# Conditioned mLSTM/retention trunk with MoE on 8 cores: eight modulation loads and eighteen weight casts are given other places in the order of work

## The chip, the cores and the metric

The kernel runs on the 8 cores of one Trainium2 chip. Each core works on one of the 8 sequences of the batch, with all weights of its own to read; nothing is exchanged between cores. The metric is the device time in microseconds of the slowest core. Three runs of the kernel before gave 3336.61, 3298.0 and 3298.25 us, with a median of 3298.25 us.

## The reference, cut to what matters

Two layers, each a mixer and then a mixture of experts (MoE). A vector `mod` of six parts per layer is computed from the condition `c` and shifts, scales and gates both halves of the layer.

```python
for l in range(2):
    mod = silu(c) @ w_ada[l] + b_ada[l]            # 1024 -> 6 * 1024
    sh1, sc1, g1, sh2, sc2, g2 = split(mod, 6)
    h = rms_norm(x, norm1_g[l]) * (1 + sc1) + sh1
    # mixer: one input projection, 4 mLSTM heads and 4 retention heads, a branch
    # projection and a sigmoid gate for each, one output projection
    x = x + g1 * hybrid_mixer(h, ...)
    h = rms_norm(x, norm2_g[l]) * (1 + sc2) + sh2
    # 4 groups x 4 experts, top-1 group, top-2 experts in it; 1024 -> 512 -> 1024
    x = x + g2 * hier_moe(h, ...)
return rms_norm(x, final_g)                         # x: 2048 tokens x 1024 per core
```

`w_ada` is 1024 x 6144 f32 per layer. The kernel treats it as 12 pieces of 512 columns, numbered 0 to 11: 0 to 3 make `sh1` and `sc1`, 4 and 5 make `g1`, 6 to 9 make `sh2` and `sc2`, and 10 and 11 make `g2`.

## The kernel before

**Order of work.** The program is straight-line code. A small scheduler (`S.op`, `S.dma`, lines 40 to 159) appends each instruction to its engine's list and puts semaphore waits before it from the buffers that it reads and writes. Each engine works through its own list in order, and so does each issuing engine with its DMAs. Every DMA that POOL issues goes into the one software queue, q0: the loads of the mixer's weights (f32 in HBM, bf16 in SBUF), the loads of `w_ada`, the casts of expert weights, and the scatters and gathers of the MoE. SP and ACT have hardware queues of their own.

**One layer.** A mixer works through two halves of 1024 tokens (`hf` 0 and 1). In each half, `run_stream([0, 1, 2, 3])` computes the four mLSTM heads in 32 slots (4 tasks x 8 chunks of 128 tokens), then `branch_proj(True, 1)` projects them in 8 steps, `run_stream([4, 5, 6, 7])` and `branch_proj(False, 1)` do the same for the retention heads, and `out_gen` does the output projection in 8 steps. That makes 88 slots a half and 176 a layer. In a stream each slot issues, by POOL, one tiny power operation (L782), so POOL keeps step with the stream; in the projections POOL waits only for weight buffers to come free (`load_w`, L501), and in `out_gen` it runs ahead. A stream's V/output-gate products are on L696; the branch projection's two products are on L843 (branch weights in `wq`) and L850 (gate weights in `wk`). `branch_proj(False, 1)` also loads the output weights, eight pieces of 256 KB, at its first two steps.

**Modulation pieces.** `ada_gen` (L866) runs beside the first stream of a half in layer 0. For each piece, POOL loads 512 columns of `w_ada` (2 MB f32 read, 1 MB bf16 written, L276) into one of two halves of `yT`, which is free at that time; PE multiplies them with silu(c) (`ada_mm`, L283, 8 products), ACT copies the row out, and PE turns it back to columns (`ada_tr`, L292). The load of piece p+2 is issued when piece p has been used. Pieces 0 to 3 of layer 0 come before the first mixer (L336). In half 0 of layer 0, pieces 4 to 11 of layer 0 are computed (8 of them), and in half 1 all 12 pieces of layer 1. In layer 1 there are none.

**Casts of the experts' weights.** The 16 experts of a layer are turned from f32 (`w_exp`) into bf16 (`ws`) in HBM beforehand, in 6 DMAs an expert (1 MB read, 512 KB written each), 96 a layer. `precast_slot` is called once in each of the 176 slots and issues (slot x 96 + 167) // 168 in all, so 0.571 a slot, with the last at slot 168.

**MoE.** After a barrier of all engines and DMAs, SP issues the prefetch of the first four experts (24 loads of 512 KB from `ws`, L994) into `ring`. Routing works on four groups of 512 tokens (`ssq`, `modul`, `router_mm`, `to_tokens`, `routing`): the normalized tokens go to `htok[0..3]` (ACT, L1088), routing computes their places, and POOL scatters each `htok` twice to HBM (L1174, 8 DMAs a group). `to_tokens` of the next group writes the same four `htok` buffers and so waits until the scatters that read them have landed. Each `S.op` in ACT's list behind that wait, the next group's `h32k` (L1064) among them, waits too. A second barrier ends the routing; then 47 blocks of 128 rows go through their experts (`wmm`, L1318), with `load_w` (L1304) bringing further experts, and rows are gathered back.

Of the kernel before, what the change touches and what calls it, by code (L numbers as in the profile page):

```python
# [23 lines left out]
RING = 4  # L24
# [172 lines left out]
def build(stop_after=None, dumps=()):  # L197
# [37 lines left out]
    with ExitStack() as st:  # L235
        S = Sched(nc, st)
# [38 lines left out]
        def ada_load(l, jg, dst, buf, extra=()):  # L275
            S.dma("pool", lambda h: h.dma_start(out=dst, in_=W_ADA[l, :, jg * 512:(jg + 1) * 512].rearrange("(k p) n -> p k n", p=128)),  # L276
                  writes=[buf] + list(extra))

        def ada_mm(l, jg, wa_, buf, bk, row, b_row):
            def mm(h):  # L280
                ins = None
                for k in range(8):
                    ins = h.matmul(bank[bk][0:1, :], lhsT=csilb[:, k:k + 1], rhs=wa_[:, k, :], start=(k == 0), stop=(k == 7))  # L283
                return ins
            S.op("pe", mm, reads=[buf, b_c], writes=[pb[bk]])
            S.op("act", lambda h: h.activation(out=row[0:1, :], in_=bank[bk][0:1, :], func=AF.Copy), writes=[pb[bk], b_row])
# [44 lines left out]
        with ExitStack() as p0:  # L331
# [3 lines left out]
            for jg in range(4):  # L335
# [5 lines left out]
                 reads=[b_c], writes=[b_c])  # L341
            S.op("dve", lambda h: h.tensor_scalar(out=csil[:], in0=csil[:], scalar1=0.5, scalar2=None, op0=ALU.mult),
                 reads=[b_c], writes=[b_c])
# [13 lines left out]
                 writes=[b_r])  # L357
# [11 lines left out]
            for t in range(16):  # L369
                S.dma("sp", lambda h, t=t: h.dma_start(out=xs[t % 4][:], in_=X[t * 128:(t + 1) * 128, :]), writes=[b_xs[t % 4]])  # L370
                for hb in range(2):
# [8 lines left out]
                    if eng == "act":  # L380
# [3 lines left out]
                            reads=[], writes=[pb[hb + 2 * (t % 2)], b_xT[t // 4]])  # L384
                    else:
# [3 lines left out]
                            reads=[], writes=[pb[hb + 2 * (t % 2)], b_xT[t // 4]])  # L389
# [14 lines left out]
        if stop_after == "p0":  # L404
            return finish(nc, S, st, final_evs, xT, b_xT, bank, pb, ident, FING, cb, mhalf, OUT, sbt)

        b_ws = [Buf("ws%d" % i) for i in range(2)]
        PCH = 6
        pc_next = [0, 0]

        def precast(l, n):
            for _ in range(n):
                i = pc_next[l]
                if i >= 16 * PCH:
                    return
                pc_next[l] = i + 1
                e, c = divmod(i, PCH)
                cw = EXPW // PCH
                ev = S.dma("pool", lambda h: h.dma_start(out=WS[l][e, :, c * cw:(c + 1) * cw], in_=W_EXP[l, e, :, c * cw:(c + 1) * cw]),
                           track=b_ws[l])  # L420
                b_ws[l].w = ev

        pc_slot = [0, 0]

        def precast_slot(l):

            pc_slot[l] += 1
            precast(l, (pc_slot[l] * 16 * PCH + 167) // 168 - pc_next[l])

        def run(*gens):  # L430

# [10 lines left out]
        for l in range(2):  # L442
            with ExitStack() as mx:
# [49 lines left out]
                for kb in (0, 4, 1, 5, 2, 6, 3, 7):  # L493
                    for j in range(4):
                        S.op("pool", lambda h: h.tensor_scalar(out=dg[:, kb, j, :], in0=identb[:], scalar1=convw[:, l, j, kb:kb + 1],
                                                               scalar2=None, op0=ALU.mult),
                             reads=[b_const, cb["convw"]], writes=[b_dg[kb]])
# [11 lines left out]
                for hf in range(2):  # L509
# [353 lines left out]
                                         reads=[b_tmp], writes=[b_yT[tg]])  # L863
                    def ada_gen():

                        todo = [(0, jg) for jg in range(4, 12)] if hf == 0 else [(1, jg) for jg in range(12)]  # L866
                        np_ = len(todo)
                        at = [3 + p * 28 // (np_ - 1) for p in range(np_)]
                        for p in range(2):
                            ada_load(*todo[p], wav[p], b_wa[p], b_yT if p == 0 else ())  # L870
                        yield
                        p = 0; q = 0
                        for i in range(33):
                            if q < p:
                                ada_tr(*todo[q], mrow, b_mrow, 3)
                                if q + 2 < np_:
                                    ada_load(*todo[q + 2], wav[q % 2], b_wa[q % 2])
                                q += 1
                            if p < np_ and i == at[p]:
                                ada_mm(*todo[p], wav[p % 2], b_wa[p % 2], 3, mrow, b_mrow)  # L880
                                p += 1
                            yield

                    def run_stream(tis, extra=()):
                        stg = {ti: make_stages(tasks[ti]) for ti in tis}
                        seq = [(ti, c) for ti in tis for c in range(8)]
                        n = len(seq)

                        def call(kind, i):
                            ti, c = seq[i]  # L890
                            stg[ti][kind](c, i)
                        extra = iter(extra)
                        next(extra, None)
                        call("A", 0)
                        call("G", 0)
                        for i in range(n):
                            ti, c = seq[i]
                            nxt = tasks[ti + 1] if ti + 1 < 8 else None
                            if c == 0:
                                if ti + 2 < 8 and ti + 2 != 5:  # L900
                                    loads_qk(tasks[ti + 2])
                                if nxt is not None:
                                    loads_vo(nxt)
                                if ti in (3, 7):
                                    branch_proj(ti == 3, 0)
                            precast_slot(l)
                            if i + 1 < n:
                                call("A", i + 1)
                            call("B", i)
                            call("Q", i)  # L910
                            if i >= 1:
                                call("M", i - 1)
                            if i >= 2:
                                call("C2", i - 2)
                            if i + 1 < n:
                                call("G", i + 1)
                            call("T", i)
                            if nxt is not None:
                                w_, t_ = PIECES[c // 2]
                                prologue_piece(nxt, w_, t_, c % 2)  # L920
                            next(extra, None)
                        call("M", n - 1)
                        call("C2", n - 2)
                        call("C2", n - 1)
                        for _ in extra:
                            pass
# [34 lines left out]
                        run((norm_gen(0), 1))  # L961
                    loads_vo(tasks[0])
                    run((gates_gen(), 1), (prologue_gen(), 2))
                    run_stream([0, 1, 2, 3], ada_gen() if l == 0 else ())
                    branch_proj(True, 1)
                    run_stream([4, 5, 6, 7])
                    branch_proj(False, 1)
# [5 lines left out]
            with ExitStack() as mo:  # L973
# [15 lines left out]
                b_wl = [[Buf("wl%d_%d" % (p, i)) for i in range(RING)] for p in range(6)]  # L989
                b_pre = [Buf("wpre%d" % i) for i in range(RING)]  # L990
                b_hsw = [Buf("hsw%d" % i) for i in range(4)]; b_hz = [Buf("hz%d" % i) for i in range(2)]
                for e in range(RING):
                    for p in range(6):
                        ev = S.dma("sp", lambda h: h.dma_start(out=ring[p][:, e, :], in_=WS[l][e, :, p * 2048:(p + 1) * 2048]),  # L994
                                   reads=[b_ws[l]], track=b_pre[e])
                        b_pre[e].w = ev

                def ldreg(h, ap, mx):
                    UID[0] += 1
# [296 lines left out]
                def load_w(b):  # L1296

                    for p in range(6):
                        def f(h):
                            if p == 0:  # L1300
                                KEEP["sp"] = [ldreg(h, btab[b:b + 1, 0:1], 15), ldreg(h, btab[b:b + 1, 2:3], 1), ldreg(h, btab[b:b + 1, 3:4], (RING - 1) * 2048)]
                                KEEP["id"] = nc.next_id()
                            (r0, ev), (r1, cd), (r2, sv) = KEEP["sp"]
                            ins = h.dma_start(out=ring[p][:].rearrange("p a n -> p (a n)")[:, bass.ds(sv, 2048)],  # L1304
                                              in_=WS[l][bass.ds(ev, 1), :, p * 2048:(p + 1) * 2048].rearrange("a p n -> (a p) n"),
                                              cond=cd, bounds_check="skip_entire_dma")
                            if p == 5:
                                free_regs(h, KEEP["id"], [r0, r1, r2])
                            return ins
                        S.dma("sp", f, reads=[b_btab, b_ws[l]] + (b_pre if b < RING else []), writes=[b_wl[p][b % RING]])  # L1310

                def wmm(h, b, out, lhs, p0, n, first, last, insl):

# [69 lines left out]
                for k in range(8):  # L1383
                    S.op("dve", lambda h: h.tensor_scalar(out=dgt[k % 2][:], in0=ident[:], scalar1=modT[:, l, 40 + k:41 + k], scalar2=None, op0=ALU.mult),
                         reads=[cb["ident"], b_mod], writes=[b_dgt[k % 2]])
                    S.op("pe", lambda h: h.matmul(bank[6 + k // 4][:, (k % 4) * 128:(k % 4 + 1) * 128], lhsT=ones32[:], rhs=dgt[k % 2][:], start=True, stop=True),
                         reads=[b_dgt[k % 2], b_const], writes=[pb[6 + k // 4]])
# [60 lines left out]
                for t in range(16):  # L1448
# [4 lines left out]
                    for hb in range(2):  # L1453
# [11 lines left out]
                        else:  # L1465
                            def f(h):
                                for k in range(4):
# [4 lines left out]
                                 writes=[pb[bk + hb], b_fj[hb], b_ft[t % 2]])  # L1472
                    if l == 1:
# [9 lines left out]
                        ev = S.dma("sp", lambda h: h.dma_start(out=OUT[tcs, :], in_=ob[t % 4][:]), reads=[b_ob[t % 4]], track=b_ob[t % 4])  # L1483
# [126 lines left out]
```

How the kernel before makes its waits and increments, by code:

```python
        def thunk():  # L106
            for s, v in waits:
                h.wait_ge(s, v)
            fn(h).then_inc(sem, 1)
# [25 lines left out]
        def thunk():  # L135
            for s, v in waits:
                h.wait_ge(s, v)
            fn(h).then_inc(dsem, 16)
# [16 lines left out]
            def thunk(h=h, waits=waits):  # L155
                for s, v in waits:
                    h.wait_ge(s, v)
```

## Time and profile before

| | |
|---|---|
| runs, us | 3336.61, 3298.0, 3298.25 (median 3298.25) |
| profiled execution, us | 3322.01 |
| its span, slowest core (core 5), us | 3320.0 |
| spans of the 8 cores, us | 3284.4 to 3320.0 |
| PE busy | 2611.8 us, 79% |
| DVE / ACT / POOL busy | 43% / 40% / 20% |
| q0 (POOL's queue), share of 16 DMA engines over the span | 52.4% |
| q1 (SP's queue) | 16.4% |

All times below are microseconds from the start of the span of core 5. Where a view shows a DMA share of 1.00, all 16 DMA engines of the core were working through packets for the whole stretch; somewhat over 1 means that packets overlap. "DMA to landing" is the time from a DMA's issue to its last byte.

### The profile page before, as it was taken

The page shows a single profiled execution, that of the slowest core. Times are in us where ns is not written, and L with a number is a line of the kernel's source. Part 1 is how long each engine was busy: PE and PEld are TensorE (multiplying, and loading weights), DVE is VectorE, ACT ScalarE, POOL GpSimd, SP SyncE. Part 2 cuts the span into 40 slices and gives each one's busy share as a digit, 9 for nine tenths or more (in the row PEclk, how much of TensorE's full clock was granted, in tenths as well). Part 3 has the DMA queues.
Part 4 walks back from the last instruction along what each step waited for, and adds up shares of the span by engine and source line. Part 5 has one row for each costly group of instructions (what it writes and reads, how often), then busy time and mean ns, then how long its engine had stood idle before and what let it go on. Part 6 is the DMA issues. An engine that isn't in the chain of part 4 may idle for free.

```text
span 3320.0 us, 56309 instructions; the slowest of 8 cores (3284.4 to 3320.0 us)
## 1 busy us (share of the span) xinstructions
PE 2611.8 (79%) x13114; PEld 1240.5 (37%) x13114; DVE 1440.6 (43%) x3484; ACT 1314.1 (40%) x2985; POOL 658.1 (20%) x1108
## 2 busy tenths in 40 slices
PE   4787886887798874688956989788988795499977
PEld 3343443343344321344433444333434331144444
DVE  3244273333446333444444555533536433354445
ACT  2465272254447133122224755624736424122224
POOL 0322132022223102000043322311323201100013
PEclk8798998898899987799976999999999998599989
DMA  8399899579989641588662788882779842358857
GB/s 194 55 136 134 116 117 125 70 98 141 132 118 117 101 163 67 174 273 267 214 238 66 112 116 129 116 132 43 113 120 127 124 124 109 115 195 295 269 185 261
DMA packets 186185, 481.55 MB, mean 145 GB/s; under 512 B 19600, under 2 KB 45072, under 8 KB 185488
## 3 DMA queue, kind: packets, MB, share of 16 engines
q0 software_dynamic: 116896, 268.51, 52.4%
q1 hardware_dynamic: 53568, 181.11, 16.4%
q10 hardware_dynamic: 15408, 28.32, 2.9%
q8 instruction: 127, 2.08, 0.3%
q14 instruction: 186, 1.52, 0.2%
HBM read 831.28 MB, written 185.60 MB: 306 GB/s over the span
## 4 chain that ended last, share of the span: by engine, by line
PE 48%; DMA 17%; issue 11%; ACT 9%; DVE 9%; SPq 4%; POOL 1%; another core or an unknown queue 0%; DVEq 0%; ACTq 0%; POOLq 0%
PE bank L1318 9%; PE bank L696 7%; PE bank L843 6%; DMA yT_u<-w_ada 5%; PE bank L850 5%; PE bank L611 4%; DMA wq_u<-w_br 4%; PE bank L942 3%; PE bank L516 2%; DMA ring_u<-ws 2%; SPq L1304 2%; SPq L1001 1%; DMA xs_u<-x 1%; PE bank L1041 1%; PE bank L1066 1%
## 5 line engine op out<-in xcount | busy, mean ns | idle before, releaser
L696 PE MATMUL bank<-wvo_u,hT_u 128*128 128x512 bf16 x2048 | 486.6, 381 | 2.5 <-DMA wvo_u<-w_in 2.5
L1318 PE MATMUL bank<-ring_u,hTb_u 128*128 x1504 | 385.6, 395 | 53.6 <-DMA ring_u<-ws 46.0
L1336 ACT ACTIVATE hTb_u<-bank 128x1024 bf16<-128x1024 bf16 x94 | 96.3, 1024 | 559.0 <-PE bank L1333 487.0
L843 PE MATMUL bank<-ymT_u,wq_u 128*128 128x512 bf16 x1024 | 263.6, 404 | 66.0 <-DMA wq_u<-w_br 54.9
L782 POOL TENSOR_TENSOR tiny_u<-tiny_u,mhalf_u 128x1 f32<-128x1 f32 x256 | 161.8, 632 | 691.4 <-DVE tiny_u L778 389.1
L696 PEld LDWEIGHTS bank<-wvo_u,hT_u 128*128 128x128 bf16 x2048 | 193.7, 98 | 229.5 <-issue 19.1
L853 ACT ACTIVATE pad_u<-bank 128x512 f32<-128x512 f32 x128 | 76.4, 597 | 464.0 <-PE bank L850 464.0
L850 PE MATMUL bank<-hT_u,wk_u 128*128 128x512 bf16 x1024 | 246.8, 385 | 1.8 <-DMA wk_u<-w_in 1.5
L1318 PEld LDWEIGHTS bank<-ring_u,hTb_u 128*128 128x128 bf16 x1504 | 146.5, 100 | 237.2 <-issue 115.7
L1426 POOL DMA_INDIRECT yg_u<-yd,gidx_u x64 | 65.4, 1022 | 715.6 <-DMA yd<-ysb_u 699.4
L1318 PE MATMUL bank<-ring_u,heT_u 128*128 x752 | 178.1, 380 | 10.2 <-DVE heT_u L1365 10.2
L843 PEld LDWEIGHTS bank<-ymT_u,wq_u 128*128 128x128 bf16 x1024 | 103.0, 102 | 201.0 <-issue 94.8
L1376 DVE TENSOR_TENSOR ysb_u<-bank,g2r_u 128x512 f32<-128x512 f32 x188 | 129.4, 689 | 52.0 <-DMA yd<-ysb_u 26.8
L850 PEld LDWEIGHTS bank<-hT_u,wk_u 128*128 128x128 bf16 x1024 | 101.9, 100 | 131.5 <-issue 18.1
L1066 PE MATMUL bank<-h32k_u,wr_s_u 128*20 128x512 f32 x128 | 84.3, 747 | 83.1 <-ACT h32k_u L1064 82.8
L611 PE MATMUL bank<-hT_u,wk_u 128*128 128x512 bf16 x512 | 129.7, 399 | 4.2 <-ACT acc_u L645 4.2
L1351 DVE SCALAR_TENSOR_TENSOR tht_u<-tht_u,bank 128x512 f32<-128x512 f32 x94 | 64.5, 687 | 155.8 <-ACT tht_u L1350 155.5
L855 DVE SCALAR_TENSOR_TENSOR yT_u<-pad_u,bank 128x512 bf16<-128x512 f32 x64 | 44.0, 687 | 200.7 <-ACT pad_u L853 200.7
L611 PE MATMUL bank<-hT_u,wq_u 128*128 128x512 bf16 x512 | 127.3, 394 | 3.7 <-ACT acc_u L645 3.7
L789 DVE SCALAR_TENSOR_TENSOR ymc_u<-bank,tiny_u,gsig_u 128x256 bf16<-128x256 f32 x256 | 122.2, 477 | 4.3 <-POOL tiny_u L782 2.9
L942 PE MATMUL bank<-yT_u,wvo_u 128*128 128x512 bf16 x512 | 121.5, 395 | 1.8 <-DVE yT_u L862 1.8
L699 ACT ACTIVATE vext_u<-bank 128x256 bf16<-128x256 f32 x256 | 96.8, 378 | 60.4 <-PE bank L696 58.3
(259 smaller groups left out, 4620.7 us busy)
## 6 DMA issues: line engine op xcount, KB each, us to landing
ring_u<-ws SPq DMA_DIRECT2D x612, 512.0 KB, 15.6
ws<-w_exp POOLq DMA_DIRECT2D x192, 512.0 KB, 12.5
yd<-ysb_u SPq DMA_DIRECT2D x94, 512.0 KB, 4.8
wvo_u<-w_in POOLq DMA_DIRECT2D x64, 512.0 KB, 10.9
wk_u<-w_in POOLq DMA_DIRECT2D x96, 256.0 KB, 6.8
hblk_u<-hs ACTq DMA_DIRECT2D x88, 256.0 KB, 4.8
yT_u<-w_ada POOLq DMA_DIRECT2D x20, 1024.0 KB, 25.0
xs_u<-x SPq DMA_DIRECT2D x16, 512.0 KB, 9.7
```

The costliest lines, as they stand in the source:

```text
L611: ins = h.matmul(bank[pbi][:], lhsT=wsel[0][wi][:, k, :], rhs=hT[:, k, lc], start=(k == 0), stop=(k == 7))
L696: ins = h.matmul(bank[vb][:], lhsT=hT[:, k, cc], rhs=wvo[wi][:, :, k, :], start=(k == 0), stop=(k == 7))
L699: S.op("act", lambda h: h.activation(out=vext[vi][:, 0:256], in_=bank[vb][:, 0:256], func=AF.Copy), writes=[pb[vb], b_v[vi]])
L782: S.op("pool", lambda h: h.tensor_tensor(out=tny[:, 7:8], in0=tny[:, 4:5], in1=mhalf[:, 0:1], op=ALU.pow), reads=[b_const], writes=[b_tny])
L789: S.op("dve", lambda h: h.scalar_tensor_tensor(out=ymc[vi][:], in0=bank[ob_][:, 0:256], scalar=tny[:, 7:8], in1=gsig[idx % 3][:], op0=ALU. ...
L843: ins = h.matmul(bank[bA][:], lhsT=wq[ji][:, k, :], rhs=ymT[:, k, lc], start=(k == 0), stop=(k == 7))
L850: ins = h.matmul(bank[bB][:], lhsT=wk[ji][:, k, :], rhs=hT[:, k, lc], start=(k == 0), stop=(k == 7))
L942: ins = h.matmul(bank[ob2][:], lhsT=wt[:, k, :], rhs=yT[:, k, lc], start=(k == 0), stop=(k == 7))
L1066: S.op("pe", lambda h: h.matmul(psLT, lhsT=wr[:, k, :], rhs=h32k[k % 2][:], start=(k == 0), stop=(k == 7)), reads=[b_h32k[k % 2], cb["wr"] ...
L1318: ins = h.matmul(out, lhsT=lhs(i), rhs=ring[p][:].rearrange("p a n -> p (a n)")[:, bass.ds(PREG[b][1] + (i % 4) * 512, 512)], start=(first ...
L1336: S.op("act", lambda h: h.activation(out=hT2[b % 2][:].rearrange("p k t -> p (k t)"), in_=psT, func=AF.Copy), writes=[pb[BT], b_hT2[b % 2]])
L1376: S.op("dve", lambda h: h.tensor_tensor(out=ysb[b % 2][:, n * 512:(n + 1) * 512], in0=bank[BY[n]][:], in1=g2r[:, n * 512:(n + 1) * 512], o ...
```

## The change

Three edits. First, the pieces of `w_ada`: half 0 of both layers now computes pieces 4 to 11 of its own layer, and half 1 of layer 0 only pieces 0 to 3 of layer 1. Eight pieces so move from half 1 of layer 0 to half 0 of layer 1; the total stays. Second, only the first 13 experts (78 casts) are cast in the mixer; the other 18 casts are issued by POOL at one go after the prefetch's place at the start of the routing stage, with a tracking buffer of their own (`b_wsl`), so that the prefetch does not wait for them; the MoE's `load_w` does. Third, `precast_slot` counts 2 a slot, but 1 in the 32 slots of the first stream of half 0, and issues (count x 78 + 319) // 320 in all. The count reaches 32 + 144 x 2 = 320 at the last slot.

```diff
-        b_ws = [Buf("ws%d" % i) for i in range(2)]
+
+        b_ws = [Buf("ws%d" % i) for i in range(2)]; b_wsl = [Buf("wsl%d" % i) for i in range(2)]
         PCH = 6
+        PCL = 13 * PCH
         pc_next = [0, 0]
 
         def precast(l, n):
...
                 ev = S.dma("pool", lambda h: h.dma_start(out=WS[l][e, :, c * cw:(c + 1) * cw], in_=W_EXP[l, e, :, c * cw:(c + 1) * cw]),
-                           track=b_ws[l])
-                b_ws[l].w = ev
+                           track=b_ws[l] if i < PCL else b_wsl[l])
+                (b_ws[l] if i < PCL else b_wsl[l]).w = ev
 
         pc_slot = [0, 0]
 
-        def precast_slot(l):
-
-            pc_slot[l] += 1
-            precast(l, (pc_slot[l] * 16 * PCH + 167) // 168 - pc_next[l])
+        def precast_slot(l, wt=2):
+
+            pc_slot[l] += wt
+            precast(l, (pc_slot[l] * PCL + 319) // 320 - pc_next[l] if pc_next[l] < PCL else 0)
...
                     def ada_gen():
 
-                        todo = [(0, jg) for jg in range(4, 12)] if hf == 0 else [(1, jg) for jg in range(12)]
+                        todo = [(1, jg) for jg in range(4)] if l == 0 and hf == 1 else [(l, jg) for jg in range(4, 12)]
...
-                            precast_slot(l)
+                            precast_slot(l, 1 if hf == 0 and tis[0] == 0 else 2)
...
-                    run_stream([0, 1, 2, 3], ada_gen() if l == 0 else ())
+                    run_stream([0, 1, 2, 3], ada_gen() if l == 0 or hf == 0 else ())
...
                         b_pre[e].w = ev
+
+                precast(l, 16 * PCH - pc_next[l])
...
-                        S.dma("sp", f, reads=[b_btab, b_ws[l]] + (b_pre if b < RING else []), writes=[b_wl[p][b % RING]])
+                        S.dma("sp", f, reads=[b_btab, b_ws[l], b_wsl[l]] + (b_pre if b < RING else []), writes=[b_wl[p][b % RING]])
```

## Rows read from the trace of the kernel before

**Rows 1.** The page: busy engines, and the chain that ended last, by line.
```profile
PE 2611.8 (79%) x13114; PEld 1240.5 (37%) x13114; DVE 1440.6 (43%) x3484; ACT 1314.1 (40%) x2985; POOL 658.1 (20%) x1108
...
PE bank L1318 9%; PE bank L696 7%; PE bank L843 6%; DMA yT_u<-w_ada 5%; PE bank L850 5%; PE bank L611 4%; DMA wq_u<-w_br 4%; PE bank L942 3%; PE bank L516 2%; DMA ring_u<-ws 2%; SPq L1304 2%; SPq L1001 1%; DMA xs_u<-x 1%; PE bank L1041 1%; 
```

**Rows 2.** Stretches: stretch, its length, busy us by engine, PE clock, DMA share, GB/s.
```profile
158.00:402.00 244.00, 202.67 (x1040) 96.42 (x1039) 92.83 (x277) 113.46 (x296) 60.35 (x119) 0.93 0.99 128
694.00:958.00 264.00, 215.81 (x1105) 102.31 (x1103) 93.01 (x283) 116.62 (x299) 65.07 (x124) 0.92 1.01 133
1834.00:2023.00 189.00, 172.46 (x911) 83.75 (x910) 91.51 (x266) 106.90 (x288) 53.93 (x112) 0.98 0.83 120
2304.00:2494.00 190.00, 172.44 (x916) 84.03 (x914) 91.74 (x266) 106.92 (x287) 54.65 (x112) 0.98 0.78 118
```

**Rows 3.** PE's waits, 150 to 340 us, and 340 to 402: total, times, longest.
```profile
PE bank L283 <- DMA yT_u<-w_ada: 22.2, 3, 9.1
...
PE bank L696 <- DMA wvo_u<-w_in: 2.5, 2, 1.5
...
PE bank L843 <- DMA wq_u<-w_bm: 8.2, 1, 8.2
```

**Rows 4.** PE's waits, 690 to 905 us.
```profile
PE bank L283 <- DMA yT_u<-w_ada: 38.3, 6, 12.5
```

**Rows 5.** PE's waits in the four retention branch projections, in order of time.
```profile
PE bank L843 <- DMA wq_u<-w_br: 21.3, 3, 12.1
...
PE bank L843 <- DMA wq_u<-w_br: 10.3, 2, 8.3
...
PE bank L843 <- DMA wq_u<-w_br: 14.8, 4, 8.6
...
PE bank L843 <- DMA wq_u<-w_br: 8.6, 3, 4.0
```

**Rows 6.** Two bursts of six casts with nothing else behind them: layer 0, then layer 1.
```profile
L419 POOL DMA_DIRECT2D ws<-w_exp x6: 515/517/529, 588.8 to 591.4; - x6
...
DMA to landing us min/median/max: 10.3/21.9/33.2
...
L419 POOL DMA_DIRECT2D ws<-w_exp x6: 515/515/529, 2201.0 to 2203.6; - x6
...
DMA to landing us min/median/max: 12.8/20.8/25.7
```

**Rows 7.** Stretches as in rows 2: cast burst, output projection, prefetch, group 0's scatters.
```profile
590.00:625.00 35.00, 30.96 (x118) 13.26 (x117) 10.17 (x15) 10.96 (x17) 4.06 (x8) 0.95 1.00 116
...
1136.00:1178.00 42.00, 40.17 (x186) 17.84 (x184) 18.37 (x26) 2.39 (x4) 0.17 (x1) 1.00 0.12 21
...
1179.00:1220.00 41.00, 29.49 (x84) 8.62 (x84) 10.22 (x21) 22.98 (x36) 0.95 (x1) 0.86 0.90 311
...
1239.00:1252.00 13.00, 7.31 (x32) 2.45 (x32) 3.31 (x9) 8.53 (x13) 8.56 (x8) 0.89 0.42 162
```

**Rows 8.** Timeline of layer 0's routing: first scatter of group 0, then ACT's copies.
```profile
1239.31 1.07 POOL L1174 DMA_INDIRECT hs<-htok_u,sidx_u  x1 [59.35 <-DVE msm_u L1061]
...
1248.61 2.81 ACT L1088 ACTIVATE htok_u<-bank 128x1024 bf16<-128x1024 bf16 x3
1251.61 1.02 ACT L1088 ACTIVATE htok_u<-bank 128x1024 bf16<-128x1024 bf16 x1 [0.20 <-issue]
```

**Rows 9.** The same in layer 1: SP's first issue, the first scatter, ACT's copies.
```profile
2711.06 0.33 SPq L985 DMA_DIRECT2D wr_s_u<-wr  x1
...
2771.91 1.05 POOL L1174 DMA_INDIRECT hs<-htok_u,sidx_u  x1 [59.71 <-DVE msm_u L1061]
...
2781.49 3.71 ACT L1088 ACTIVATE htok_u<-bank 128x1024 bf16<-128x1024 bf16 x4
```

**Rows 10.** Start of the program: four loads of POOL's queue against sixteen of SP's.
```profile
L276 POOL DMA_DIRECT2D wa_u<-w_ada x4: 911/928/1078, 1.6 to 4.4; - x4
...
DMA to landing us min/median/max: 17.7/38.0/60.9
```

## The prediction

> **What bounds the kernel now.** I read the page first. PE is busy 79% of the span, and the chain that ended last lies mostly on PE's products, but two DMAs stand in it with 5% and 4%: the loads of `w_ada` and of `w_br` [rows 1]. So some stretches wait for POOL's software queue. The view by stretches shows which. The same work, an mLSTM stream and its branch projection, takes 244 us in half 0 of layer 0 (8 modulation pieces), 264 in half 1 (12 pieces), and 189 and 190 in layer 1 (none). The DMA engines are full in the first two (0.99, 1.01) and not in the others (0.83, 0.78), and PE's clock falls from 0.98 to 0.93 and 0.92 with the waits [rows 2]. The waits name the cause: PE stood 22.2 us for `w_ada` and 10.7 for weights queued behind it in half 0, and 38.3 in half 1 [rows 3, 4]. The retention projections add four waits for `w_br`, 21.3, 10.3, 14.8 and 8.6 us, 55 in all [rows 5]. A stream of this kind hides about 150 us of DMA; what is piled on top makes it longer.
>
> **Fewer pieces beside layer 0's streams.** DMA time is share times length: 242 and 267 us with pieces, 157 and 148 (mean 152) without [rows 2]. A piece is then (242 - 152) / 8 = 11 or (267 - 152) / 12 = 10 us; I take 10. A cast is bounded by the two bursts: (591.4 + 33.2 - 588.8 - 10.3) / 5 = 5.1 us in layer 0 and, worked the same way, 3.1 in layer 1 [rows 6]; mean 4.1. The 40 slots of such a stretch carried 22.9 casts. With the new counts they carry 32 x 0.244 + 8 x 0.4875 = 11.7 in half 0 and 19.5 in half 1.
>
> A piece also costs PE and ACT something when its data is there. Half 0 is 55 us longer than 189, of which 33 are the waits of rows 3; 22 / 8 = 2.8 us. Half 1 is 75 longer, less 38 of waits; 37 / 12 = 3.1. I take 2.9.
>
> Half 0 of layer 0 keeps 8 pieces but sheds 11.2 casts (46 us at 4.1): 242 - 46 = 196 us of DMA for a stretch of 189 + 8 x 2.9 = 212, a share of 0.92. The queue no longer sets the pace: 244 to 212, **-32**. Half 1 keeps 4 pieces: 152 + 40 - 3.4 x 4.1 = 178 us of DMA in 189 + 12 = 201: 264 to 201, **-63**. Half 0 of layer 1 takes 8 pieces: 157 + 80 - 46 = 191 of DMA in 189 + 23 = 212, share 0.90: **+23**. Its upper bound is what 8 pieces cost now with casts at full pace, +55; the lower is nothing. Sum of the three: -72. The PE, ACT and DVE work of the pieces is only moved and is in the 2.9; g1, the second scale and g2 of layer 1 are needed only in its output projection and later.
>
> **Slower pace elsewhere.** A retention stream of 32 slots carries 15.6 casts in place of 18.3, 11 us less of queue ahead of the first `w_br` load. The eight output weights, 2 MB, still stand ahead of the third. Of the 55 us [rows 5] between nothing and 40 can go; I take **-15**, nearer the low end because the output weights are not moved. The casts that this shifts into the last output projection, 4 of them, cost nothing: the DMA engines stand at 0.12 there [rows 7]. If that cover failed, the barrier would come 4 x 5.1 = 20 us later.
>
> **Eighteen casts at the start of routing.** POOL needs 18 x 0.52 = 9 us to issue them [rows 6] and has nothing else until the first scatter 60 us later [rows 8, 9], so the issuing is free. SP's queue: the 24 prefetch loads fill the engines for 0.90 x 41 = 37 us [rows 7]. They are needed only after the second barrier, so their being slowed costs nothing, and nothing that routing waits for is behind them on SP; the small router weights are issued ahead of them.
>
> What is not free is the software queue. The eight scatters of group 0, issued from 1239.3 on, now stand behind all 18 casts, and ACT's four copies of group 1 into `htok`, done at 1252.6, wait for them [rows 8]. Behind those copies, in ACT's list, is the whole of group 2's modulation, and behind that PE and DVE. The DMA engines have 18c us of casts, c each, and 37 of prefetch to do first. That these add, and do not overlap, is seen at the start of the program: four `w_ada` loads against SP's sixteen loads of `x` land (4.4 + 60.9 - 1.6 - 17.7) / 3 = 15.3 us apart, not 10 [rows 10]. The scatters themselves take 0.42 x 13 = 5.5 us [rows 7] and the last copy 1. So the copies end at 1179 + 18c + 37 + 6.5, later than now by 18c - 30; in layer 1, from 2711.1 to 2785.2 [rows 9], the same 18c - 30. Nothing later makes this up, since group to group is one chain. Before it the queue was empty at that point. With the bounds of rows 6 the delay is 26 us (3.1) to 62 us (5.1) a layer; nothing at all if the prefetch were hidden behind the casts. I take 4.6 in layer 0, nearer its own burst, and 4.0 in layer 1: 53 + 42 = **+95**. Later scatter groups find the queue empty again.
>
> The Trainium skill ("DMA: Bandwidth & Descriptors", section on the anatomy of one SWDGE DMA) fits a DMA of this path as 2.0 us plus bytes over 436 GB/s. For the 1 MB that a cast reads this is an estimate of 2.4 us each in a full queue, by which the delay would be 13 us a layer and the sum -61. The bursts of rows 6 do not bear that rate out.
>
> **Sum.** -32 - 63 + 23 - 15 + 95 = +8 us. The profiled execution took 3322 us, 24 above the median of the runs, 3298. So +8 is 3330 in its terms and **3306** in the median's.
>
> **The rivals.** All times in the median's terms. What this measurement can tell from no change is about 2%, 66 us.
>
> *A, faster: scatters find the queue nearly empty.* The casts run at layer 1's 3.1 us or better and the prefetch hides in their gaps, 56 us in all, over before 1239. For it: layer 1's burst, and the routing stage has empty DMA time before the scatters. Against: the burst of layer 0 at 5.1 with the engines at 1.00 [rows 6, 7]. Then only the mixers' -87 remains: 3211. With the additive rule it needs c under 2.2.
> The Trainium skill's 2.4 us would give 3237; its page "HBM Reference" (Specifications) speaks the other way, giving each core of a streaming pair half of 716 GB/s, an estimate of 4.4 us for the 1.5 MB that a cast reads and writes.
>
> *B, slower: the burst is dearer than any seen.* Place: group 1's copies in both layers. All eight cores cast and prefetch at once, after a barrier that comes at about the same time on each, which no burst of rows 6 did. At 6.5 us a cast the delay is 87 a layer: +174 - 87 = +87, 3385. It decides from 18c - 30 > 76, c over 5.9. Against: 5.1 was already with full engines.
>
> *C, layer 1's first half turns into layer 0's.* The eight pieces there cost the +55 that they cost now, because a piece waits for its own turn in the queue however free the mean is. For: the load of piece p+2 is issued only when piece p is used. Against: the shares of about 0.9 worked out above. Sum +40: 3338.
>
> That the change does not do what it says I exclude by the diff: 96 casts and 24 pieces stay, and the count of 320 gives 78.
>
> **How the numbers follow.** Main case 0.60: its bounds are c from 3.1 to 5.1 in both layers (52 to 124 for routing) and mixers of -75 to -105, so 3245 to 3347. A 0.15, C 0.15, B 0.08, and 0.02 for the mixers gaining nothing. The range is 3240 to 3355; it holds the main case and C and leaves out most of A and B. Faster by over 2% (under 3232) is most of A and a little of the main case's edge: 0.15. Slower by over 2% (over 3364) is B and a little of C: 0.09. Within: 0.76.
>
> **What would show it.** Right: mLSTM stretches of about 212, 201, 212 and 189 us, DMA shares under 0.95 in each, hardly any PE wait for `w_ada`; ACT's second group of `htok` copies ending some 53 and 42 us later after the first barrier than now, with a DMA share near 1 from the barrier to the scatters, and PE idle there. Wrong: copies of group 1 on time (A), casts over 5.9 us apart in routing (B), PE waits of 20 us or more for `w_ada` in layer 1 (C), or a retention projection that waits as long as before.

## The result

The changed kernel took 3358.78 us (median of 5 runs, 3340.53 to 3507.92), the kernel before beside it 3312.8 us. In some runs of either kernel a die shows a lower granted clock and the run is a few per cent longer; the ratios, here and below, leave such runs out. The ratio is 1.0126, 95% interval 1.0065 to 1.0188. So the change costs 21 to 62 us, near 42. The forecast was +8, in a range of -58 to +57.

The profile after shows two large movements that nearly cancel. First the page: PE's and ACT's work is unchanged, and the share of POOL's queue falls from 52.4% to 49.0%.

```profile
span 3356.8 us, 56324 instructions; the slowest of 8 cores (3289.8 to 3356.8 us)
...
PE 2604.0 (78%) x13114; PEld 1239.7 (37%) x13114; DVE 1442.2 (43%) x3484; ACT 1311.8 (39%) x2985; POOL 653.3 (19%) x1108
...
q0 software_dynamic: 116896, 268.51, 49.0%
```

**The mixers gained what was forecast.** Stretches of the changed kernel, columns as in [rows 2]: the four mLSTM streams with their branch projections, then the two stretches from the last output product to the first expert product.

```profile
157.00:369.00 212.00, 199.97 (x1039) 96.86 (x1037) 92.97 (x277) 112.48 (x295) 54.97 (x109) 0.95 0.85 120
652.00:854.00 202.00, 186.73 (x976) 90.59 (x975) 92.07 (x272) 109.77 (x291) 55.15 (x112) 0.97 0.88 123
1794.00:2001.00 207.00, 195.24 (x1038) 95.32 (x1036) 92.86 (x277) 112.52 (x296) 54.35 (x108) 0.98 0.81 123
2283.00:2476.00 193.00, 174.41 (x916) 84.74 (x915) 91.94 (x266) 107.12 (x288) 51.63 (x108) 0.97 0.67 107
1070.00:1321.00 251.00, 96.47 (x306) 28.94 (x306) 68.07 (x234) 65.20 (x98) 42.05 (x51) 0.67 0.63 142
2689.00:2930.00 241.00, 99.65 (x307) 29.94 (x305) 68.58 (x234) 65.30 (x98) 41.98 (x51) 0.66 0.64 147
```

Against 244, 264, 189 and 190 us [rows 2] the four are 212, 202, 207 and 193, with DMA shares of 0.67 to 0.88 where two were full. PE's wait for `w_ada` [rows 3, 4] is gone. Its waits for `w_br`, in order of time, are 39 us in place of 55 [rows 5]:

```profile
PE bank L845 <- DMA wq_u<-w_br: 11.4, 3, 6.8
...
PE bank L845 <- DMA wq_u<-w_br: 8.1, 2, 6.0
...
PE bank L845 <- DMA wq_u<-w_br: 11.8, 3, 8.3
...
PE bank L845 <- DMA wq_u<-w_br: 7.6, 2, 6.9
```

**Routing lost more than that.** The last two stretches were 185 and 184 us on the slowest core before. The timeline of ACT in the changed kernel, layer 0 and then layer 1 (start, length, and in brackets ACT's idle time before), answers to [rows 8, 9]:

```profile
1141.90 0.57 ACT L1081 ACTIVATE lgT_u<-bank 20x512 f32<-20x512 f32 x1
1195.74 1.02 ACT L1092 ACTIVATE htok_u<-bank 128x1024 bf16<-128x1024 bf16 x1 [53.27 <-DMA hs<-htok_u,sidx_u]
1198.46 1.02 ACT L1092 ACTIVATE htok_u<-bank 128x1024 bf16<-128x1024 bf16 x1 [1.70 <-DMA hs<-htok_u,sidx_u]
...
1203.57 1.02 ACT L1092 ACTIVATE htok_u<-bank 128x1024 bf16<-128x1024 bf16 x1 [1.64 <-DMA hs<-htok_u,sidx_u]
...
2811.95 1.02 ACT L1092 ACTIVATE htok_u<-bank 128x1024 bf16<-128x1024 bf16 x1 [49.34 <-DMA hs<-htok_u,sidx_u]
...
2819.78 1.02 ACT L1092 ACTIVATE htok_u<-bank 128x1024 bf16<-128x1024 bf16 x1 [1.64 <-DMA hs<-htok_u,sidx_u]
```

ACT stands for 53.3 and 49.3 us before its first copy of group 1, each time for a scatter, and again 1.4 to 1.7 us before each further one. The DMA engines are full meanwhile and PE is nearly idle (8 of 66 us), at a granted clock of 0.58 of its 2.4 GHz:

```profile
1072.00:1130.00 58.00, 40.98 (x122) 11.25 (x122) 20.77 (x61) 28.69 (x46) 10.29 (x20) 0.90 0.96 158
1130.00:1196.00 66.00, 8.18 (x32) 2.63 (x32) 3.28 (x8) 5.40 (x10) 8.24 (x8) 0.58 0.99 185
```

What the readings below rest on is one table, worked out from the first and last products of each stage in the one trace of each kernel, as the median of the 8 cores. "mL" is an mLSTM stream with its projection, "ret" the same for retention, a and b the two halves, "rout" the stretch from the last output product to the first expert product.

```
                        layer 0                              layer 1
                    mL a  ret a  mL b  ret b  rout     mL a  ret a  mL b  ret b  rout   slowest span
before             243.5  197.1 262.4  187.0 181.8    189.1  192.7 189.8  187.2 183.4    3320.0
after              210.3  188.5 202.4  184.7 240.6    210.5  186.3 192.8  184.1 234.9    3356.8
all in mixer       212.0  192.7 210.6  189.7 181.5    210.5  192.8 192.1  188.5 182.5    3254.2
pieces only        237.9  195.5 205.5  185.3 183.5    232.9  192.6 192.0  187.1 182.3    3324.0
late prefetch      208.8  191.1 202.4  185.0 209.5    209.7  187.8 192.7  184.7 201.2    3287.6
spread             208.8  188.2 202.4  184.7 188.0    210.0  185.5 192.8  184.7 186.3    3228.1
burst of 9         212.1  191.0 202.5  188.0 190.4    208.6  187.9 189.9  187.3 188.6    3254.5
spread, old places 210.4  188.2 248.5  184.0 186.8    189.8  187.7 189.6  184.0 187.3    3257.1
spread 14          212.1  191.3 202.4  185.1 184.2    208.5  186.8 192.2  184.4 184.0    3255.2
```

From before to after, the eight mixer columns sum to -89.2 and the two routing columns to +110.3. A single trace moves by some us without any edit: the spread kernel, traced a second time, gave 190.1 and 188.3 us of routing in place of 188.0 and 186.3.

### The profile page after: what moved, and what is told of

Read it like the earlier page. It is cut to its first block, busy times and chain, and to the rows that moved or that the text cites. A ratio compares the mean times of both kernels' runs of the same rounds, so it can differ in the third digit from the quotient of the medians.

```text
span 3356.8 us, 56324 instructions; the slowest of 8 cores (3289.8 to 3356.8 us)
## 1 busy us (share of the span) xinstructions
PE 2604.0 (78%) x13114; PEld 1239.7 (37%) x13114; DVE 1442.2 (43%) x3484; ACT 1311.8 (39%) x2985; POOL 653.3 (19%) x1108
## 4 chain that ended last, share of the span: by engine, by line
PE 49%; issue 11%; DMA 10%; ACT 10%; DVE 9%; another core or an unknown queue 5%; SPq 5%; DVEq 1%; ACTq 0%; POOL 0%; POOLq 0%
PE bank L698 7%; PE bank L1322 7%; PE bank L845 6%; PE bank L852 6%; PE bank L613 5%; PE bank L944 3%; DMA wq_u<-w_br 3%; DMA yd<-ysb_u 3%; DMA ring_u<-ws 2%; PE bank L518 2%; SPq L1308 2%; PE bank L283 2%; SPq L1005 1%; PE bank L644 1%
## 5 line engine op out<-in xcount | busy, mean ns | idle before, releaser
L1322 PE MATMUL bank<-ring_u,hTb_u 128*128 x1504 | 378.1, 388 | 59.5 <-DMA ring_u<-ws 51.8
L698 PEld LDWEIGHTS bank<-wvo_u,hT_u 128*128 128x128 bf16 x2048 | 193.7, 98 | 222.6 <-issue 10.7
L1070 PE MATMUL bank<-h32k_u,wr_s_u 128*20 128x512 f32 x128 | 88.2, 779 | 190.1 <-ACT h32k_u L1068 189.4
L1178 POOL DMA_INDIRECT hs<-htok_u,sidx_u x64 | 63.9, 998 | 366.2 <-DVE msm_u L1065 313.7
L421 POOL DMA_DIRECT2D ws<-w_exp x192 | 105.9, 554 | 90.9 <-issue 88.5
```

What stands on the lines that cost most here:

```text
L698: ins = h.matmul(bank[vb][:], lhsT=hT[:, k, cc], rhs=wvo[wi][:, :, k, :], start=(k == 0), stop=(k == 7))
L1070: S.op("pe", lambda h: h.matmul(psLT, lhsT=wr[:, k, :], rhs=h32k[k % 2][:], start=(k == 0), stop=(k == 7)), reads=[b_h32k[k % 2], cb["wr"] ...
L1322: ins = h.matmul(out, lhsT=lhs(i), rhs=ring[p][:].rearrange("p a n -> p (a n)")[:, bass.ds(PREG[b][1] + (i % 4) * 512, 512)], start=(first ...
```

## The experiments

**All casts in the mixer.** Undoes the burst alone.

```diff
-        PCL = 13 * PCH
+        PCL = 16 * PCH
```

> All 96 casts stay in the mixer (0.6 a slot, 0.3 beside the eight-piece streams), none at the start of routing; the moved modulation pieces and the half pace stay. Queue theory (the loss is group 1's copies waiting for scatters that stand behind 18 casts): the stretch from the last output product to the first expert product goes back to 184 to 190 us in both layers, 123 us less than in the changed kernel, and the mixers take 5 to 20 us more for the 18 casts; about 3240 us, 55 to 70 below the kernel before. Rival (the mixers' gain comes only from having 18 fewer casts, and the moved pieces give nothing net): mixers as long as before, about 3290 us.

Measured: 3255.24 us (3250.14 to 3262.41), ratio to before 0.9823 (0.9781 to 0.9865). Routing is back at 181.5 and 182.5 us, and the mixers take 29 us more than in the changed kernel for 18 more casts (the eight columns summed), more than the 5 to 20 expected. The rival falls: the mixers stay 60 us shorter than before with all 96 casts in them. Putting 18 casts in a burst turned a gain of 1.8% into a loss of 1.3%.

**The pieces alone.** The kernel before with the `todo` line and the `run_stream` line of the change, nothing else.

```diff
-                        todo = [(0, jg) for jg in range(4, 12)] if hf == 0 else [(1, jg) for jg in range(12)]
+                        todo = [(1, jg) for jg in range(4)] if l == 0 and hf == 1 else [(l, jg) for jg in range(4, 12)]
...
-                    run_stream([0, 1, 2, 3], ada_gen() if l == 0 else ())
+                    run_stream([0, 1, 2, 3], ada_gen() if l == 0 or hf == 0 else ())
```

> The kernel before with the eight modulation pieces moved and nothing else: casts at full pace, all in the mixer. Theory (a stretch is long where its DMA time exceeds what the stream hides): half 1 of layer 0 falls from 264 to 201 to 206 us, half 0 of layer 1 rises from 189 to about 240, as half 0 of layer 0 is now, and half 0 of layer 0 stays at 244; net -10, about 3290 us. Rival (moving the pieces is the whole gain and the pace of casts does nothing): half 0 of layer 1 rises to 212 only, net -40, about 3258 us.

Measured: 0.9954 (0.9914 to 0.9993), some 15 us below before; 3312.52 us as the median of all its 11 runs. Half 1 of layer 0 falls by 56.9 us and half 0 of layer 1 rises by 43.8, close to the theory. Half 0 of layer 0, whose code is the same as before, reads 237.9 us in place of 243.5, so a difference of 6 us in such a full stretch says nothing. The wait for `w_ada` is back in layer 1, in the view of PE's waits there:

```profile
PE bank L283 <- DMA yT_u<-w_ada: 17.6, 2, 10.6
...
PE bank L843 <- DMA wq_u<-w_bm: 2.1, 1, 2.1
```

Against "all in mixer", which differs only in the pace of casts, the two eight-piece stretches are 25.9 and 22.4 us longer. Over the eight mixer columns the moved pieces alone give 20 us (5.6 of them in that unchanged stretch) and the new pace another 40; the pieces need the pace, or their new place fills up as the old one did.

**Prefetch after group 1's copies.** The changed kernel, the burst kept.

```diff
-                for e in range(RING):
+                def prefetch():
+                    for e in range(RING):
...
-                                   reads=[b_ws[l]], track=b_pre[e])
...
+                                       reads=[b_ws[l], b_T1], track=b_pre[e])
...
                 precast(l, 16 * PCH - pc_next[l])
+                b_T1 = Buf("t1")
...
                     to_tokens(g)
+                    if g == 1:
+                        b_T1.w = b_htok[3].w
+                        prefetch()
```

> The changed kernel, with SP's 24 prefetch loads issued only after group 1's copies instead of at the barrier; the burst of 18 casts stays. Theory that casts and prefetch add up on the DMA engines: group 1's copies come 37 us a layer earlier than in the changed kernel, still some 20 us later than before; in all 65 to 75 us less than the changed kernel, about 3280 us. Rival (the scatters wait for the casts alone, and the prefetch runs beside them for nothing): no change, 3350 us. The prefetch must still be done before the first expert product; if not, that product comes later.

Measured: 3284.28 us, 0.988 (0.9827 to 0.9933) of before. Routing falls to 209.5 and 201.2, by 31.1 and 33.7 us, 65 in all where 65 to 75 were expected. The burst and ACT's first two copies of group 1, layer 0, of this kernel, in the views by tile and by time:

```profile
L421 POOL DMA_DIRECT2D ws<-w_exp x18: 515/515/518, 1062.6 to 1072.5; - x18
```

```profile
1147.44 1.02 ACT L1094 ACTIVATE htok_u<-bank 128x1024 bf16<-128x1024 bf16 x1 [15.08 <-DMA hs<-htok_u,sidx_u]
1150.67 1.02 ACT L1094 ACTIVATE htok_u<-bank 128x1024 bf16<-128x1024 bf16 x1 [2.21 <-DMA hs<-htok_u,sidx_u]
```

From the burst's first issue to the first copy are 84.8 us here (core 1), and in the changed kernel (core 0) 1195.7 - 1072.0 = 123.7. These are two different cores; over all eight the medians are 85.8 and 119.0 us, in layer 1 82.2 and 115.0. So the prefetch, estimated at 37, costs the first copy 33 us a layer (38.9 between these two cores), and the rival that it runs beside the casts for nothing is out. Less two scatters (2.7 us, the distance of copies that each wait for a pair) the 18 casts alone take 83 us, 4.6 each, and 79.5 in layer 1, 4.4 each.

It doesn't follow that the scatters stood behind the whole prefetch. Packets, MB and share of the engines by queue (q0 is POOL's, q1 SP's) are, in the changed kernel from 1080 to 1180 us and from its first copy on (1195.7 to 1210), and then in this kernel from 1071 to 1141:

```profile
q0 software_dynamic: 2257, 8.21, 62.2%
q1 hardware_dynamic: 2252, 8.20, 36.7%
...
q1 hardware_dynamic: 566, 2.03, 34.7%
...
q0 software_dynamic: 2192, 8.00, 99.3%
```

With both queues loaded, each moved the same 8.2 MB in 100 us, 0.082 MB a us. POOL's alone moved 8.0 MB in 70 us, 0.114 MB a us. A cast (0.52 MB written) so lasts 6.4 us beside the prefetch and 4.6 without it. And when the first copy began, 2.03 of the prefetch's 12.7 MB were still to come. The burst is slowed while SP's queue has work, by what that queue moves meanwhile.

**The casts spread over routing.** The same 18 casts, 4 at the barrier and the rest behind the scatters of groups 0, 1 and 2.

```diff
-                precast(l, 16 * PCH - pc_next[l])
+                precast(l, 4)
...
                         run((routing(g), 5), *nxt)
+                        precast(l, (6, 5, 3)[g])
```

> The changed kernel with its 18 late casts not in one burst: 4 at the start of routing, then 6, 5 and 3 behind the scatters of groups 0, 1 and 2. The number of casts and their bytes in the routing stage are the same. Queue theory: no group of copies waits more than some 5 us, the stretch falls from 251 and 241 us to 190 to 195 in each layer, about 100 us less than the changed kernel, 3245 us. Rival (any DMA load of this size slows the routing stage, through memory or the clock): 60 us or less is won, 3290 us or more.

Measured: 3246.13 us, 0.9797 (0.9749 to 0.9845). Routing takes 188.0 and 186.3 us with the same bytes in it, so neither memory nor clock nor the amount of DMA in the stage was the cause, but when the casts stand in the queue. ACT's waits for scatters over the whole run, the changed kernel and then this one:

```profile
ACT htok_u L1092 <- DMA hs<-htok_u,sidx_u: 112.1, 8, 53.3
```

```profile
ACT htok_u L1092 <- DMA hs<-htok_u,sidx_u: 16.1, 11, 2.7
```

**A burst of 9.** The changed kernel with `PCL = 87`.

> The changed kernel with 87 casts in the mixer and a burst of 9 in place of 18 at the start of routing. Queue theory: the delay of group 1's copies is a constant plus 4.8 us a cast (what the changed kernel's trace gives), so the stretch from the last output product to the first expert product falls by 9 x 4.8 = 43 us a layer, to about 197 and 192 (medians of the cores, from 241 and 235); the mixers take about 5 us more; about 3275 us. Rival (a burst costs by being there: the queue's switch, the slowed prefetch, the clock): about half of the loss stays, stretches of about 211 and 209, 3305 us.

Measured: one run of 3256.45 us with a profile, too few for a ratio. Routing takes 190.4 and 188.6 us, below the 197 and 192 expected: nine casts fewer took away 50 and 46 us. The rival, that half of the cost comes with any burst, is out. The burst, the first scatter and ACT's first copy of group 1 in layer 0, then the two queues from 1081 to 1131 us:

```profile
L421 POOL DMA_DIRECT2D ws<-w_exp x9: 515/515/517, 1073.6 to 1079.0; - x9
...
1132.64 1.07 POOL L1178 DMA_INDIRECT hs<-htok_u,sidx_u  x1 [52.14 <-DVE msm_u L1065]
...
1143.18 1.02 ACT L1092 ACTIVATE htok_u<-bank 128x1024 bf16<-128x1024 bf16 x1 [0.91 <-issue]
...
q0 software_dynamic: 1178, 4.30, 61.3%
q1 hardware_dynamic: 1174, 4.28, 38.0%
```

The first copy comes 69.6 us after the first cast (68.0 to 72.0 over the eight cores and both layers), as early as with the casts spread (68.7 to 70.9). If casts and the whole prefetch had to be done first, it would come after 9 x 4.6 + 33 + 2.7 = 77 us at the least. At the pace beside the prefetch ((119 - 2.7) / 18 = 6.5 us a cast in the changed kernel) nine casts last 58 us and are about over when the first scatter is issued, 59 us after the first cast, while SP's queue is still at work. So the two loads don't simply add. What is left of the cost is that the scatters land beside the rest of the prefetch: the four copies of group 1 start over 8.9 and 8.0 us in place of 3.1 and 2.9.

**Spread casts, pieces in their old places.** The spread kernel with the `todo` and `run_stream` lines of the kernel before.

> The spread kernel (casts of 4, 6, 5 and 3 in routing) with the modulation pieces back in their old places: 12 in half 1 of layer 0, none in layer 1. Theory that a stretch lasts as long as its DMA time where that is longer: half 1 of layer 0 needs 152 + 120 - 14 = 258 us of DMA, so it goes from 202 to 245 to 258, and half 0 of layer 1 from 210 to 189; net 25 to 35 more than the spread kernel, about 3275 us. Rival (with the casts relieved the places no longer matter): within 10 us of the spread kernel, 3246 us.

Measured: 3261.49 us, 0.9852 (0.9786 to 0.9918). Half 1 of layer 0 takes 248.5 us, inside the 245 to 258 worked out from its DMA time, and PE waits for `w_ada` again:

```profile
PE bank L283 <- DMA yT_u<-w_ada: 28.0, 4, 9.8
```

Half 0 of layer 1 is 20.2 us shorter than in the spread kernel. The moved pieces are worth 46.1 - 20.2 = 26 us by these two stretches; the times themselves (intervals that overlap) don't separate the two kernels.

**Four casts more under the output projection, 14 spread.** The spread kernel with

```diff
                             precast_slot(l)
+                            if hf == 1 and j == 7:
+                                precast(l, 4)
...
-                        precast(l, (6, 5, 3)[g])
+                        precast(l, (4, 4, 2)[g])
```

> The spread kernel with four of its 18 late casts issued at the last step of the second half's output projection, where the DMA engines stand near 0.1, and 4, 4, 4 and 2 in routing. Theory: the routing stretch falls from 188 and 186 to about 184 a layer, and the barrier is not later; 5 to 8 us less, 3240 us. Rival: the four casts (with the four already there, 8 x 4.1 = 33 us in a stretch of 42) land after the last product and the barrier comes later by as much: no gain or 5 us more.

Measured: two runs, 3239.73 and 3256.76 us, too few for a ratio; routing 184.2 and 184.0 us, as expected. Both spread kernels were run again beside each other.

> The same kernel as the one with 14 casts spread in routing and four at the end of the output projection, since its first rounds gave too few undisturbed runs. By the stretches of its profile (184 us in routing in both layers, against 188 and 186) it should stand at or up to 8 us below the spread kernel, about 3240 us; if it stands above it, the four casts cost elsewhere.

> The spread kernel again, on the same chip and beside the same runs of the kernel before: 3245 us, 0.980 of the kernel before.

Measured: 14 spread 3236.23 us (3227.44 to 3241.0), 0.9765 (0.9738 to 0.9793); 18 spread 0.9825 (0.9777 to 0.9873), from three runs of 3251.21 to 3262.31. The first beats the kernel before, by about 78 us, and the changed one. That it beats the other spread kernel is likely: the intervals overlap, but each of its six runs is shorter than each of the three. Its routing took 184.6 and 183.5 us in this second trace.

Not tried: enough `htok` buffers that no copy waits for a scatter.

## Why the prediction was right, and where its sum was off

**The streams.** -32, -63 and +23 were forecast; the stretches moved by -33, -60 and +21 in the median. The price of a piece (2.9 us of PE and ACT, 10 of DMA) and the rule that a stretch lasts as long as the longer of its two sums held in both directions: with 12 pieces and slow casts it gave 248.5 where 245 to 258 were worked out. C, that layer 1's first half turns into layer 0's, did not happen, since casts at half pace left room; in the experiment with the pieces alone it did (232.9).

**The retention projections.** -15 forecast; the four columns sum to -20, and the waits fell from 55 to 39 us. A second-half mLSTM stretch in layer 1 rose by 3 us, which had no term.

**The routing stage.** The chain was right: the scatters stand behind the burst, ACT's copies behind the scatters, everything else behind the copies. On the median core the copies of group 1 end 55.4 and 51.4 us later than before, where 53 and 42 were forecast, and the stretches grow by 110 instead of 95. The terms of 18c - 30 were these. The cast: 4.6 us alone in layer 0, as taken, but 4.4 in layer 1 where I took 4.0; averaging a fast and a slow burst was no ground for a burst in which all cores cast. The scatters: I took 5.5 us for all eight from the DMA share of a stretch in which they had trickled in, but the copies that wait for them come 2.6 us apart, so eight take 10.5. The prefetch: 33 us where I took 37.

That this last term came out near is luck. "Casts and prefetch have to be done first" is wrong: the two queues share the engines, and the burst waits only for what SP's queue moves while the burst lasts. Eighteen casts last so long that by their end most of the prefetch has gone (10.7 of 12.7 MB by the first copy, and that share of 37 us is 31), so the two rules give nearly the same; with nine casts they part, and the addition puts the first copy 7 us late or more. The start of the program [rows 10], 15.3 us a load instead of 10, fits sharing as well as adding, since SP's loads ran all the while.

On the slowest core, 0, the two stretches grow by 66 + 57 = 123 us over those of core 5 before. After the copies of layer 0 core 0 needed 116 us to the first expert product where core 5 had needed 109, which had no term; in layer 1 it did not. Before, too, this part took from 106 to 113 us by core. What makes it differ stays open.

**The slowest core.** Between the two profiled executions the slowest cores are 37 us apart: -88 in the eight mixer stretches, +123 in routing, +1 in the rest. The median of the eight cores rose by only 12, from 3303 to 3315. Much of this difference is the scatter of single executions. The slowest core stood 17 us above the median core in the profiled execution before and 41 in the one after, but 23 and 20 in the other two runs behind the ratio, and 11 to 53 (mean 25) in 21 such runs of the kernel before. By these runs the median core went from 3285 (3277 to 3299) to 3315, 3322 and 3319, a rise of 34 us. The table's columns give 21 of them; where the other 13 lie isn't shown, as each kernel was traced once. In the trace after, the routing stretches do differ more by core: 234 to 251 us in layer 0 and 225 to 242 in layer 1, where 181 to 188 and 183 to 187 stood before. Why some cores are served slower in the burst was not tested.

**The sum.** With the median stretches as measured the sum is -89 + 110 = +21 in place of +8, and the measured time is +42. The mixers' terms hit and the routing term was 15 short; that the time still fell in the range is owed to its width, for the error of 34 us is larger than the forecast itself.

**The rivals.** A and B fell with the delays, 55 and 51 us, where A needs under 10 and B over 76. In the prediction's terms, c alone was 4.6 and 4.4 us, between the 2.2 and 5.9 from which they would decide. The sign given for B, casts over 5.9 us apart in routing, would have misled: beside the prefetch they were 6.5 apart, without B being true.

## What to carry to other kernels

A load that is moved to where the DMA engines stand idle is free only if nothing that the stage waits for is issued later into the same queue. Count what stands ahead of the first waited-for transfer in its own queue, at the pace that it has beside the other loaded queues, against the time until it is issued; here 18 casts lasted some 116 us against 60, 9 casts 58 us and didn't delay the first copy, and the same 18 casts in four portions cost 4 to 7 us a layer against none in routing. Work put beside a stage should be sized stretch by stretch: DMA time against compute time, with the longer one as the forecast.

## What the runs showed that was not expected

SP's prefetch was held up in its issuing too: with the burst beside it one of its first 15 issues took 16.9 us, where the longest of all 24 in layer 0 before was 3.6, and the quickest load landed after 12.2 us in place of 6.0 (6.9 to 12.7 over the cores). View of the tile `ring`, changed kernel:

```profile
L996 SPq DMA_DIRECT2D ring_u<-ws x15: 424/934/16926, 1072.2 to 1108.8; - x15
...
DMA to landing us min/median/max: 12.2/35.5/67.5
```

Nothing that routing waits for is issued by SP behind these loads, so the held issues themselves cost nothing here. What an issue waits for is not shown; that SP's queue was full is a guess.
